# Expert rows of two tables gathered as one row of 8192 bytes, in a hybrid decoder step on one core

## The chip, the core and the metric

One core of a Trainium2 chip (trn2) runs the whole program once. The metric is the device time in microseconds.

## What is computed

One decoder layer for a prompt of 1024 tokens and for 64 sample tokens (8 sequences of 8): norm, one projection, attention over a latent cache (for the samples over 32 pages of 128 rows each), a pooling mixer, a gated merge, and then `peer`, the expert part around which the change turns. All is float32.

```
q = (xt @ peer_w_q).reshape(n_tok, 8, 2, 128)
s = einsum('nhpd,hpkd->nhpk', q, peer_keys)
s_top, i_top = top_k(s, 16)
cand = s_top[..., 0, :, None] + s_top[..., 1, None, :]
best, pos = top_k(cand.reshape(n_tok, 8, 256), 16)
expert = take_along_axis(i_top[..., 0, :, None] * 128 + i_top[..., 1, None, :], pos)
gate = softmax(best)
a = gelu(einsum('td,ted->te', x, peer_u[expert]))
y = einsum('te,ted->td', gate * a, peer_v[expert])
```

Each token has 8 heads of 16 experts; a row of `peer_u` or `peer_v` is 1024 floats.

## The kernel before, in words

The prompt's eight tiles of 128 tokens go through in three groups of 2, 3 and 3 tiles (class `Prompt`); group 0 runs alone, then the other two, the page attention of the samples (class `Pages`, 64 groups of four pages, seven slots each) and the samples' own tail (class `Sample`) run interleaved with the experts. The order on each engine is written out by hand: `Experts` yields one slot at a time on each engine, and `main.to(slot)` runs the generator up to a slot and returns the engine for a piece of other work. There are NU = 1088 slots: 8 tiles of 128 and one half tile (64). `Plan` sets the slots of the prompt's pieces.

`Route` finds the experts of a unit (one head of 32 rows of each of four row groups, 68 units in all): on DVE `top_eight`, `top_sixteen`, `pairs`, `experts` (L1693 to L1757), on ACT the softmax (L1691). A unit is due every 16 slots.

In a slot k, POOL gathers 128 rows of `peer_u` into a ring of 8 tiles (L1820, queue of POOL); DVE multiplies and sums them with the token rows `xrep` (`dot`, L1933), which frees the ring slot. `xrep` holds a token's row on four partition groups; ACT copies it (`replicate`, L1905), five buffers. After 16 dots DVE prepares the gelu (`gelu_in`, L1942 to L1948), ACT takes one tanh (L1916), and DVE makes the weights (L1956) and one 128x512 product, the diagonals of sixteen slots (L1963). Twenty slots after u (LAG), `peer_v` rows are gathered into a ring of 11, in POOL's order behind the `peer_u` gather of that slot, and PE multiplies them with the diagonals into PSUM, four slots at a time (L1891); its last matmul frees the v slots. `collect` (L1974) adds the rest once a tile.

In the page groups PE transposes a page (L2120), ACT copies it (L2216), PE makes keys (L2134), ACT squares them (L2229), DVE sums the squares (L2290) one slot later; `new_maximum` (L2322 to L2328) and `accumulate` (L2338, L2340) keep the running maximum. Of prompt and sample, L1196 is the projection by the peer weights (`in_w_peer`).

What sets the order around the change: DVE's `diagonals` of chunk u stands at slot 16(u+1)+1; PE's matmuls of slots q to q+3 at slot q+23.

Of the kernel before, what the change touches and what calls it, by code (L numbers as in the profile page):

```python
# [14 lines left out]
P = 128  # L15
# [57 lines left out]
TOP = 52400  # L73
# [1583 lines left out]
class Route:  # L1657


    def __init__(self, env, sem):  # L1660
# [56 lines left out]
    def pairs(self):  # L1717
# [16 lines left out]
    def experts(self, dve, u):  # L1734
# [11 lines left out]
        v.tensor_tensor(h4, h4, self.topf.unsqueeze(2).to_broadcast([P, 2, TOPK, TOPK]), ALU.mult)  # L1746
# [13 lines left out]
class Experts:  # L1760


    XBUF = 5

    def __init__(self, env, sem, ps, rt):
# [14 lines left out]
        self.u_at = w  # L1780
        self.u_ring = take(RING, D)
        self.spare = w
        self.v_ring = take(VRING, D)
        self.diag = take(DIAGS, 16, 32)
        self.a, self.a2, self.th, self.wt = take(2, 16), take(16), take(16), take(16)
# [3 lines left out]
        self.u_in, self.v_in = [sem(f"i_u_in{j}") for j in range(RING)], [sem(f"i_v_in{j}") for j in range(VRING)]
        self.u_used, self.v_used = sem("i_u_used"), [sem(f"i_v_used{j}") for j in range(4)]  # L1790
        self.x0_in, self.xt_in, self.x_set, self.h_in = sem("i_x0_in"), sem("i_xt_in"), sem("i_x_set"), sem("i_h_in")
        self.act_in, self.tanh_done, self.diag_done, self.collected = (sem("i_" + n) for n in ("act_in", "tanh", "diag", "collected"))
# [3 lines left out]
        for q in range(NU):  # L1796
            at[q % self.width(q)] += 1
            self.v_count.append(at[q % self.width(q)])
            if q % 128 == 127 or q == NU - 1:
                self.tile_counts.append(tuple(at))  # L1800
# [18 lines left out]
    def gather(self, ring, slot, col, table, done):  # L1819
        self.nc.gpsimd.indirect_dma_start(out=ring[:, slot, :], out_offset=None, in_=self.I[table],  # L1820
                                          in_offset=bass.IndirectOffsetOnAxis(ap=self.ids[:, col:col + 1], axis=0)).then_inc(done[slot], 16)

    def gather_v(self, q):

        w = self.width(q)
        t, r = q // 128, q % 128 // w
        self.gather(self.v_ring, q % VRING, self.column(t, r // TOPK, q % w, r % TOPK), "peer_v", self.v_in)

    def pool(self, pool):
        for k in range(SLOTS):  # L1830
            if k < NU:
                col = self.column(*self.place(k))
                if k == 0:
                    pool.wait_ge(self.sets_used, H + 7)
                if col % TOPK == 0:
                    pool.wait_ge(self.rt.done, col // TOPK + 1)
                if k == 12:
                    pool.wait_ge(self.sets_used, 3 * H)
                    for q in range(VRING):
                        self.gather_v(q)  # L1840
# [831 lines left out]
```

## Time and profile before

| | |
|---|---|
| median of 3 runs | 3795.91 us (3793.19 to 3797.08) |
| profiled execution, span | 3792.2 us |
| instructions | 45054 |
| gathers | 2176, half of `in_peer_u`, half of `in_peer_v` |
| DMA | 1387.36 MB, mean 366 GB/s |

The profiled execution's own time is its span and the start and end around it; of the three runs the nearest, 3793.19 us, lies 1.0 us above the span. The page gives busy time and share of the span by engine; waits and the chain are inferred from semaphores. Times in the rows below are us from the span's start unless marked ns.

### The profile page before, as it was taken

How to read it: one execution, taken by the hardware profiler on the slowest of the kernel's cores; microseconds unless marked ns; L12 is line 12 of the kernel's file. 1: busy time of each engine (PE TensorE's matmuls, PEld its weight loads, DVE VectorE, ACT ScalarE, POOL GpSimd, SP SyncE). 2: the span in 40 equal slices, each digit the busy share in tenths (PEclk: the TensorE clock that was granted, in tenths of full speed). 3: DMA queues.
4: the chain of work that ended last, by engine and by line, in shares of the span. 5: the costliest groups of instructions: out<-in, count | busy, mean ns of one | idle time of the engine just before them, and what ended most of it. 6: DMA issues, size and time to landing. Idle time of an engine off the chain costs nothing.

```text
span 3792.2 us, 45054 instructions
## 1 busy us (share of the span) xinstructions
PE 2995.8 (79%) x13427; PEld 1568.6 (41%) x13427; DVE 2673.4 (70%) x6884; ACT 954.4 (25%) x1899; POOL 2417.9 (64%) x2196
## 2 busy tenths in 40 slices
PE   8998878986797889987688888888888886566345
PEld 5775335533342554443344444444444443423001
DVE  2426887664578876665688988889888987554753
ACT  1211222200123320210245344434453434000100
POOL 0004556764675777665777777777777877666776
PEclk9998978998997889998799999899999998776668
DMA  6456999999999999999999999999999999999999
GB/s 223 109 196 245 334 315 366 412 409 379 368 388 354 382 373 412 409 412 367 382 374 396 390 367 387 373 398 375 385 392 393 375 393 398 413 412 407 409 391 371
DMA packets 434388, 1387.36 MB, mean 366 GB/s; under 512 B 60954, under 2 KB 119291, under 8 KB 429731
## 3 DMA queue, kind: packets, MB, share of 16 engines
q0 software_dynamic: 313344, 1140.99, 77.4%
q1 hardware_dynamic: 120802, 243.49, 18.1%
q8 instruction: 110, 1.80, 0.2%
q14 instruction: 132, 1.07, 0.1%
HBM read 1354.17 MB, written 30.11 MB: 365 GB/s over the span
## 4 chain that ended last, share of the span: by engine, by line
PE 26%; DVE 25%; DMA 20%; POOL 12%; issue 8%; DVEq 4%; ACT 2%; SPq 1%; ACTq 0%; POOLq 0%
POOL arena L1820 12%; DMA arena<-in_peer_v,arena 9%; DVE arena L1933 8%; DMA arena<-in_peer_u,arena 6%; PE ps L1891 5%; PE ps L863 4%; PE ps L2134 3%; PE ps L1196 3%; DVE arena L2290 2%; DMA arena<-in_w_peer 2%; PE ps L813 1%; PE ps L1034 1%; DMA arena<-s_dram 1%; ACT arena L1905 1%; PE ps L1011 1%
## 5 line engine op out<-in xcount | busy, mean ns | idle before, releaser
L1820 POOL DMA_INDIRECT arena<-in_peer_u,arena x1088 | 1215.7, 1117 | 828.7 <-PE ps L1174 300.3
L1933 DVE CUSTOM_DVE_ANT_0 arena<-arena 128x1024 f32<-128x1024 f32 x1088 | 1317.2, 1222 | 444.7 <-DMA arena<-in_peer_u,arena 419.3
L1820 POOL DMA_INDIRECT arena<-in_peer_v,arena x1088 | 1200.7, 1104 | 507.6 <-issue 301.5
L1891 PE MATMUL ps<-arena 128*32 128x512 f32 x4352 | 663.2, 697 | 345.7 <-DMA arena<-in_peer_v,arena 338.8
L2134 PE MATMUL ps<-arena 128*128 128x512 f32 x1056 | 544.6, 640 | 14.9 <-ACT arena L2229 12.9
L1891 PEld LDWEIGHTS ps<-arena 128*32 128x32 f32 x4352 | 141.5, 121 | 713.1 <-issue 706.5
L1196 PE MATMUL ps<-arena 128*128 128x384 f32 (+2 forms) x896 | 250.9, 433 | 53.2 <-DMA arena<-in_w_peer 53.1
L2229 ACT ACTIVATE arena<-ps 128x512 f32<-128x512 f32 x264 | 157.8, 598 | 445.4 <-PE ps L2134 426.8
L2134 PEld LDWEIGHTS ps<-arena 128*128 128x128 f32 x1056 | 191.3, 202 | 177.8 <-issue 167.7
L2142 PEld LDWEIGHTS ps<-arena 128*128 128x128 f32 x1056 | 167.0, 199 | 139.3 <-issue 137.6
L2290 DVE TENSOR_REDUCE arena<-arena 128x8 f32<-128x512 f32 x264 | 180.3, 683 | 49.3 <-ACT arena L2229 37.4
L1196 PEld LDWEIGHTS ps<-arena 128*128 128x128 f32 x896 | 154.8, 199 | 135.7 <-issue 81.1
L2165 PE MATMUL ps<-arena 128*64 128x257 f32 x528 | 140.3, 413 | 65.1 <-ACT arena L2249 65.1
L863 PE MATMUL ps<-arena 128*128 128x384 f32 (+1 forms) x528 | 172.1, 486 | 23.8 <-DVE arena L1452 23.8
L1103 PE MATMUL ps<-arena 128*128 128x384 f32 x512 | 171.5, 489 | 0.0
L2216 ACT ACTIVATE arena<-ps 128x256 f32<-128x256 f32 (+1 forms) x264 | 107.4, 407 | 247.5 <-PE ps L2120 196.8
L2142 PE MATMUL ps<-arena 128*128 128x64 f32 x1056 | 151.9, 268 | 0.0
L1905 ACT ACTIVATE arena<-arena 32x1024 f32<-32x1024 f32 x120 | 126.4, 1053 | 76.5 <-DVE arena L1933 68.3
L863 PEld LDWEIGHTS ps<-arena 128*128 128x128 f32 x528 | 103.5, 198 | 93.3 <-issue 36.9
L2120 PE MATMUL ps<-const,arena 128*128 128x128 f32 x528 | 114.0, 299 | 22.8 <-ACTq L2219 14.9
L1103 PEld LDWEIGHTS ps<-arena 128*128 128x128 f32 x512 | 96.0, 190 | 77.7 <-issue 14.1
L2165 PEld LDWEIGHTS ps<-arena 128*64 128x64 f32 x528 | 71.4, 145 | 117.3 <-ACT arena L2249 77.9
(239 smaller groups left out, 3774.7 us busy)
## 6 DMA issues: line engine op xcount, KB each, us to landing
arena<-in_w_peer SPq DMA_DIRECT2D x64, 576.0 KB, 7.8
arena<-in_w_merge SPq DMA_DIRECT2D x24, 1536.0 KB, 9.5
arena<-in_cache SPq DMA_DIRECT2D x256, 144.0 KB
arena<-in_peer_u,arena POOLq DMA_INDIRECT x1088, 8.5
arena<-in_peer_v,arena POOLq DMA_INDIRECT x1088, 8.7
arena<-in_w_front SPq DMA_DIRECT2D x33, 512.0 KB, 6.7
arena<-in_w_out SPq DMA_DIRECT2D x24, 512.0 KB, 8.9
arena<-s_dram SPq DMA_DIRECT2D x68, 128.0 KB
```

What stands on the lines that cost most here:

```text
L863: last = t.matmul(bank, w[:, k, :], xnT[:, k, :], start=k == 0, stop=k == KD - 1)
L1103: last = t.matmul(ps[:, 2 + 2 * (d % 2) + a, 0:T], ring[:, a * KD + k, :], xnT[:, k, 0:T], start=k == 0, stop=k == KD - 1)
L1196: last = t.matmul(ps[:, 2 + e % 2, lo * P:hi * P], self.p_item(g, j)[:, k, :], xn2T[:, k, lo * P:hi * P], start=k == 0, stop=k == KD - 1)
L1820: self.nc.gpsimd.indirect_dma_start(out=ring[:, slot, :], out_offset=None, in_=self.I[table], in_offset=bass.IndirectOffsetOnAxis(ap=self. ...
L1891: mm = self.nc.tensor.matmul(self.acc[32 * j:32 * j + 32, n, :], self.diag[:, (q0 + j) // 16 % DIAGS, (q0 + j) % 16, :], self.v_ring[:, (q ...
L1905: last = self.nc.scalar.activation(self.xrep[jg % self.XBUF][32 * i:32 * i + 32, :], self.rows[32 * j:32 * j + 32, :], ACT.Copy)
L1933: self.nc.vector.tensor_tensor_reduce(out=u, in0=u, in1=self.xrep[jg % self.XBUF], scale=1.0, scalar=0.0, op0=ALU.mult, op1=ALU.add, accum ...
L2134: last = t.matmul(self.key, self.cTp[:, j % 2, k * P:(k + 1) * P], self.wuk[:, k, :], start=k == 0, stop=k == 1)
L2142: last = t.matmul(out, self.cTp[:, j % 2, k * P:(k + 1) * P], self.qlat[:, k, b * NS:b * NS + NS], start=j + k == 0, stop=False)
L2165: last = self.nc.tensor.matmul(self.acc_ps[0:NS, 0:KL + 1], self.scs[gi % 2][:, j, :], self.source(j, par)[:, 0:KL + 1], start=j == 0, sto ...
L2229: self.nc.scalar.activation(self.sqp[:, j % 2, :], self.key, ACT.Square).then_inc(self.ksq_done, 1)
L2290: self.nc.vector.tensor_reduce(out=self.ssn[:, j, :], in_=self.sqp[:, j % 2, :].rearrange("p (h d) -> p h d", h=H), axis=AX, op=ALU.add).t ...
```

## The change

The two expert tables become one, `in_peer_uv`, with rows of 2048 floats. POOL gathers both halves of an expert at once into one ring of 10 tiles of 2048 (`ring`, `pair_in`); the slot is freed only by PE's matmul. The order of the experts within a tile changes (`place`): four neighbouring slots are now the four row groups. Gelu, tanh and weights are made every four slots (CHUNK), and the diagonals by four ACT copies with a per-partition scale. LAG falls from 20 to 2: PE's matmuls of slots 4c to 4c+3 stand at slot 4c+5, after DVE's weights at 4c+4 and ACT's diagonals at 4c+5. `xrep` has 8 buffers, and ACT fills them 36, 30, 24 and 18 slots ahead. The gathers' descriptor memory shrinks from 16384 to 4096 bytes a partition, which the arena gets. In the route, ids and positions stay whole numbers; the page groups' maximum is one combined product and maximum, kept in two columns in turn. The first ten gathers wait for the prompt's steps whose buffers they overwrite. The samples share semaphores with the prompt.

The changed lines:

```diff
@@ -32,10 +32,11 @@
-RING = 8
-VRING = 11
-DIAGS = 3
-LAG = 20
+GELU_CUBE = 0.044715
+RING = 10
+CHUNK = 4
+DIAGS = 4
+LAG = 2
@@ -70,7 +71,8 @@
-TOP = 52400
+SCRATCH = 4096
+TOP = 52400 + (16384 - SCRATCH) // 4
@@ -1718,10 +1720,8 @@
-        v.tensor_copy(self.topf, self.topi)
-        v.tensor_scalar(self.topf[:, 0, :], self.topf[:, 0, :], float(NK), None, ALU.mult)
@@ -1737,19 +1737,16 @@
-        v.tensor_copy(self.hilof, self.hilo)
-        v.drain()
-        v.tensor_tensor(self.hit, self.hilof.rearrange("p a b -> p (a b)").unsqueeze(2).to_broadcast([P, 2 * TOPK, TOPK]),
+        v.tensor_tensor(self.hit, self.hilo.rearrange("p a b -> p (a b)").unsqueeze(2).to_broadcast([P, 2 * TOPK, TOPK]),
-        v.tensor_tensor(h4, h4, self.topf.unsqueeze(2).to_broadcast([P, 2, TOPK, TOPK]), ALU.mult)
+        v.tensor_tensor(h4, h4, self.topi.unsqueeze(2).to_broadcast([P, 2, TOPK, TOPK]), ALU.mult)
-        v.tensor_tensor(self.ef, self.e2[:, 0, :], self.e2[:, 1, :], ALU.add)
-        v.drain()
-        v.tensor_copy(self.ids[:, u * TOPK:(u + 1) * TOPK], self.ef)
+        v.scalar_tensor_tensor(out=self.ids[:, u * TOPK:(u + 1) * TOPK], in0=self.e2[:, 0, :], scalar=float(NK), in1=self.e2[:, 1, :],
+                               op0=ALU.mult, op1=ALU.add)
@@ -1760,7 +1757,7 @@
-    XBUF = 5
+    XBUF = 8
@@ -1777,26 +1774,24 @@
...
+        self.u_at, self.spare = w, w + 8 * D
+        self.ring = take(RING, 2 * D)
+        self.diag = take(DIAGS, CHUNK, 32)
+        self.a, self.a2, self.th, self.wt = take(2, CHUNK), take(CHUNK), take(CHUNK), take(2, CHUNK)
...
@@ -1808,42 +1803,32 @@
...
+        t, r = k // 128, k % 128
+        return t, r // (TOPK * w), r % w, r % (TOPK * w) // w
...
+    def sets_before(self, k):
+        end = 2 * D * (k + 1)
+        last = min((end - 1) // (9 * P), 6) if end <= 8 * D else min(7 + (end - 8 * D - 1) // (9 * P), 2 * H - 1)
+        return last + 9
...
+                t, m, j, s = self.place(k)
+                col = self.column(t, m, j, s)
+                if k < RING:
+                    pool.wait_ge(self.sets_used, self.sets_before(k))
+                else:
+                    pool.wait_ge(self.v_used[(k - RING) % self.width(k - RING)], self.v_count[k - RING])
+                if s == 0:
...
+                self.nc.gpsimd.indirect_dma_start(out=self.ring[:, k % RING, :], out_offset=None, in_=self.I["peer_uv"],
+                                                  in_offset=bass.IndirectOffsetOnAxis(ap=self.ids[:, col:col + 1], axis=0)).then_inc(self.pair_in[k % RING], 16)
@@ -1876,22 +1860,22 @@
...
+            c, at = divmod(k - LAG, CHUNK)
+            if c >= 0 and at == CHUNK - 1:
+                k0 = c * CHUNK
+                t, r, w = k0 // 128, k0 % 128, self.width(k0)
+                if r == 0:
...
+                pe.wait_ge(self.diag_done, c + 1)
+                for q0 in range(0, CHUNK, w):
+                    for n in range(2):
+                        for j in range(w):
+                            q = q0 + j
+                            mm = self.nc.tensor.matmul(self.acc[32 * j:32 * j + 32, n, :], self.diag[:, c % DIAGS, q, :],
+                                                       self.ring[:, (k0 + q) % RING, D + n * 512:D + (n + 1) * 512],
+                                                       start=r + q0 == 0, stop=r + q0 + w == (128 if t < PT else 64))
+                            if n:
+                                mm.then_inc(self.v_used[j], 1)
@@ -1900,7 +1884,7 @@
-            act.wait_ge(self.u_used, 128 * t0 + 112 + 4 * j0 + 4)
+            act.wait_ge(self.dotted, 128 * t0 + 124 + j0 + 1)
@@ -1909,14 +1893,15 @@
...
+            c, at = divmod(k, CHUNK)
+            if at == CHUNK - 1 and k < NU:
+                act.wait_ge(self.act_in, c + 1)
+                self.nc.scalar.activation(self.th, self.th, ACT.Tanh, scale=0.7978845608028654 * GELU_CUBE).then_inc(self.tanh_done, 1)
+            if at == 1 and 1 <= c <= NU // CHUNK:
+                self.diagonals(act, c - 1)
+            t = (k + 36) // 128
...
+                for j, ahead in enumerate((36, 30, 24, 18)):
@@ -1924,45 +1909,46 @@
...
+        if t and k % 128 < self.width(k):
...
+        dve.wait_ge(self.pair_in[k % RING], 16 * (k // RING + 1))
+        u = self.ring[:, k % RING, 0:D]
...
+                                            accum_out=self.a[:, k // CHUNK % 2, k % CHUNK:k % CHUNK + 1]).then_inc(self.dotted, 1)
...
+        v.scalar_tensor_tensor(out=self.th, in0=self.a2, scalar=1.0 / GELU_CUBE, in1=a, op0=ALU.add, op1=ALU.mult)
...
+        v.scalar_tensor_tensor(out=self.a2.rearrange("p (s j) -> p s j", j=w), in0=a.rearrange("p (s j) -> p s j", j=w), scalar=0.5,
+                               in1=self.gates[:, col:col + TOPK * w].rearrange("p (j s) -> p s j", j=w)[:, s:s + n, :], op0=ALU.mult, op1=ALU.mult)
+    def weights(self, dve, c):
...
+        need(dve, self.diag_done, c - 1)
+        v.scalar_tensor_tensor(out=self.wt[:, c % 2, :], in0=self.th, scalar=1.0, in1=self.a2, op0=ALU.add, op1=ALU.mult).then_inc(self.weights_done, 1)
+    def diagonals(self, act, c):
+        act.wait_ge(self.weights_done, c + 1)
...
+            k0 = CHUNK * (c - DIAGS)
+            for j in range(self.width(k0)):
+                act.wait_ge(self.v_used[j], self.v_count[k0 + CHUNK - self.width(k0) + j])
+        for q in range(CHUNK):
+            last = self.nc.scalar.activation(self.diag[:, c % DIAGS, q, :], self.C["stack"], ACT.Copy, scale=self.wt[:, c % 2, q:q + 1])
+        last.then_inc(self.diag_done, 1)
@@ -1976,13 +1962,13 @@
...
+                if at == CHUNK - 1:
+                    self.gelu_in(c)
+            if at == 0 and 1 <= c <= NU // CHUNK:
+                self.weights(dve, c - 1)
@@ -2241,7 +2228,7 @@
...
+        self.nc.scalar.activation(self.corr, self.m[(gi + 1) % 2], ACT.Exp, bias=self.m[gi % 2], scale=-1.0).then_inc(self.corr_done, 1)
@@ -2319,12 +2306,11 @@
...
+        mnew = self.m[(gi + 1) % 2]
+        v.tensor_tensor_reduce(out=self.held, in0=self.maxT[gi % 2], in1=self.C["ones"][0:NS, :], scale=1.0, scalar=self.m[gi % 2],
+                               op0=ALU.mult, op1=ALU.max, accum_out=mnew)
+        v.drain()
+        v.tensor_scalar(self.diag, self.C["ident"][0:NS, 0:NS], mnew, None, ALU.mult)
@@ -2335,13 +2321,12 @@
-        v.tensor_copy(self.m, self.mnew)
-    def divide(self, dve, b):
+    def divide(self, dve, b, following):
@@ -2650,9 +2636,9 @@
-        "peer_u": A["peer_u"][0], "peer_v": A["peer_v"][0],
+        "peer_uv": np.concatenate([A["peer_u"][0], A["peer_v"][0]], axis=1),
-    nc = bacc.Bacc("TRN2", target_bir_lowering=False, num_devices=1)
+    nc = bacc.Bacc("TRN2", target_bir_lowering=False, num_devices=1, dynamic_dma_scratch_size=SCRATCH)
```

(A line of "..." marks what is left out; removed lines of functions printed above are left out too.) On POOL, 12 gathers of u, 11 of v and then both in turn became 436 gathers of `in_peer_uv`, the memsets of the page groups, and 652 more.

The order on DVE before, beside the page groups, from the gelu's first step (L1942 to L1948) into the route's `experts` (L1737 to L1752):

```order
L1942 TENSOR_TENSOR arena<-arena 128x16
L1944 TENSOR_SCALAR arena<-arena 128x16
L1946 TENSOR_TENSOR arena<-arena 128x16
L1948 SCALAR_TENSOR_TENSOR arena<-arena 128x16
L1737 TENSOR_SCALAR arena<-arena 128x16
L1738 TENSOR_SCALAR arena<-arena 128x16
L1740 CAST arena<-arena 128x32
L1742 TENSOR_TENSOR arena<-arena,const 128x512
L1746 TENSOR_TENSOR arena<-arena 128x512
L1748 TENSOR_REDUCE arena<-arena 128x32
L1750 TENSOR_TENSOR arena<-arena 128x16
L1752 CAST arena<-arena 128x16
```

In it the gelu is 16 wide and comes once in 16 slots; the route makes two casts and one addition around its wide products.

The order on DVE with the change, at the same unit (gelu L1927 to L1931, route L1737 to L1748):

```order
L1927 TENSOR_TENSOR arena<-arena 128x4
L1929 SCALAR_TENSOR_TENSOR arena<-arena 128x4
L1931 SCALAR_TENSOR_TENSOR arena<-arena 128x4
L1737 TENSOR_SCALAR arena<-arena 128x16
L1738 TENSOR_SCALAR arena<-arena 128x16
L1740 TENSOR_TENSOR arena<-arena,const 128x512
L1744 TENSOR_TENSOR arena<-arena 128x512
L1746 TENSOR_REDUCE arena<-arena 128x32
L1748 SCALAR_TENSOR_TENSOR arena<-arena 128x16
```

The gelu is one step shorter, 4 wide and comes every four slots; the casts are gone, and one combined step writes the ids.

The order on ACT before, at a softmax and tanh beside the page groups, with what each row waits for (d_ names are the page groups', i_ the experts', h_ the route's; L2216 copies a page, L2229 squares keys, L1916 is the tanh):

```order
L1691 ACT_TABLE_LOAD [waits h_done]
L1691 ACTIVATE arena<-arena 128x16 [waits h_best]
L1916 ACTIVATE arena<-arena 128x16 [waits i_act_in]
L2216 ACTIVATE arena<-ps 128x256 [waits d_s,d_t_done]
L2229 ACTIVATE arena<-ps 128x512 [waits d_ks,d_key]
L2216 ACTIVATE arena<-ps 128x256 [waits d_s,d_t_done]
```

In sixteen slots this tanh is all that ACT waits for from the experts.

The order on ACT with the change (L2203 copies a page, L2216 squares keys, L1950 are the diagonals):

```order
L2216 ACTIVATE arena<-ps 128x512 [waits d_ks,d_key]
L1950 ACTIVATE arena<-const,arena 128x32 [waits i_v_used2,i_v_used1,i_v_used3,i_v_used0,i_weights]
L1950 ACTIVATE arena<-const,arena 128x32 x3
L2203 ACTIVATE arena<-ps 128x256 [waits d_s,d_t_done]
L2216 ACTIVATE arena<-ps 128x512 [waits d_ks,d_key]
L2203 ACTIVATE arena<-ps 128x256 [waits d_s,d_t_done]
```

The four diagonals wait for DVE's weights, every four slots, and stand ahead of the next page copy and square.

## Rows read from the trace of the kernel before

**Rows 1.** The page: busy time by engine; busy tenths of DMA in 40 slices.

```profile
PE 2995.8 (79%) x13427; PEld 1568.6 (41%) x13427; DVE 2673.4 (70%) x6884; ACT 954.4 (25%) x1899; POOL 2417.9 (64%) x2196
...
DMA  6456999999999999999999999999999999999999
```

**Rows 2.** Stretches, us: engine busy (x instructions), clock, DMA share, GB/s.

```profile
1400.00:1750.00 350.00, 313.02 (x1215) 157.37 (x1208) 219.69 (x540) 43.32 (x72) 237.15 (x216) 0.96 1.03 411
...
1850.00:3140.00 1290.00, 1087.84 (x5144) 548.77 (x5145) 1141.90 (x3073) 561.62 (x1095) 988.45 (x858) 0.95 1.01 384
...
3140.00:3590.00 450.00, 256.18 (x1437) 131.42 (x1435) 272.95 (x681) 53.56 (x110) 313.06 (x292) 0.71 1.03 408
```

**Rows 3.** Groups on DVE, 1850 to 3140: count | busy, mean ns | idle, releaser.

```profile
L1933 DVE CUSTOM_DVE_ANT_0 arena<-arena 128x1024 f32<-128x1024 f32 x430 | 521.8, 1220 | 10.5 <-issue 2.0
...
L2290 DVE TENSOR_REDUCE arena<-arena 128x8 f32<-128x512 f32 x253 | 172.8, 683 | 41.6 <-ACT arena L2229 30.3 <-issue 0.5
```

**Rows 4.** The dots: 311:600, 1100:1400, 600:900, 1400:1750, 3140:3760.

```profile
L1933 DVE CUSTOM_DVE_ANT_0 arena<-arena 128x1024 f32<-128x1024 f32 x78 | 93.8, 1222 | 10.7 <-DMA arena<-in_peer_u,arena 8.1 <-issue 1.6
...
L1933 DVE CUSTOM_DVE_ANT_0 arena<-arena 128x1024 f32<-128x1024 f32 x93 | 111.5, 1219 | 2.3 <-issue 1.8
...
L1933 DVE CUSTOM_DVE_ANT_0 arena<-arena 128x1024 f32<-128x1024 f32 x90 | 109.1, 1224 | 74.2 <-DMA arena<-in_peer_u,arena 72.2 <-issue 1.0
...
L1933 DVE CUSTOM_DVE_ANT_0 arena<-arena 128x1024 f32<-128x1024 f32 x106 | 128.6, 1223 | 95.5 <-DMA arena<-in_peer_u,arena 93.8 <-issue 1.1
...
L1933 DVE CUSTOM_DVE_ANT_0 arena<-arena 128x1024 f32<-128x1024 f32 x210 | 255.3, 1224 | 219.4 <-DMA arena<-in_peer_u,arena 215.0 <-issue 2.4
```

**Rows 5.** The chain of waits, 3140 to 3590, by line.

```profile
by line: DMA arena<-in_peer_v,arena 40.0%; POOL arena L1820 29.3%; issue 11.2%; PE ps L1891 7.1%; DMA arena<-in_peer_u,arena 3.4%; PE ps L2502 3.3%; DVE arena L1933 2.1%; ACT arena L1905 1.3%; PE ps L2134 1.2%; DVE arena L2290 0.3%; ACT L22
```

**Rows 6.** Waits of POOL, 1850 to 3140: us in total, times, longest.

```profile
POOL arena L1820 <- issue: 251.5, 822, 1.0
...
POOL arena L1820 <- DVE arena L1933: 44.1, 28, 3.1
```

**Rows 7.** Timeline of DVE: start us, us, line, operation.

```profile
2621.68 0.08 DVE L1933 DVE_READ_ACCUMULATOR2_ANT arena<- 128x1 f32 x1
...
2622.11 0.17 DVE L1944 TENSOR_SCALAR arena<-arena 128x16 f32<-128x16 f32 x1
...
2622.35 0.17 DVE L1946 TENSOR_TENSOR arena<-arena 128x16 f32<-128x16 f32 x1
...
2622.75 0.17 DVE L1737 TENSOR_SCALAR arena<-arena 128x16 uint32<-128x16 uint32 x1
...
2631.22 0.08 DVE L1933 DVE_READ_ACCUMULATOR2_ANT arena<- 128x1 f32 x1
...
2632.43 0.42 DVE L2333 TENSOR_TENSOR arena<-arena,ps 128x256 f32<-128x256 f32 x1
```

**Rows 8.** Timeline of DVE: first instruction of the maximum, first after it.

```profile
2626.73 0.28 DVE L2322 TENSOR_REDUCE arena<-ps 64x1 f32<-64x128 f32 x1
...
2627.74 0.69 DVE L2290 TENSOR_REDUCE arena<-arena 128x8 f32<-128x512 f32 x1
```

**Rows 9.** Groups on ACT, whole span.

```profile
L1905 ACT ACTIVATE arena<-arena 32x1024 f32<-32x1024 f32 x120 | 126.4, 1053 | 76.5 <-DVE arena L1933 68.3 <-issue 6.9
...
L1916 ACT ACTIVATE arena<-arena 128x16 f32<-128x16 f32 x68 | 14.4, 212 | 414.2 <-DVEq L1947 414.1
```

**Rows 10.** Stretches again, one of 75 us, while merge weights load.

```profile
3270.00:3345.00 75.00, 40.58 (x288) 27.83 (x288) 40.05 (x113) 1.61 (x7) 44.35 (x43) 0.74 1.02 415
```

**Rows 11.** Timeline, all engines, end of the program.

```profile
3760.90 0.21 ACT L1916 ACTIVATE arena<-arena 128x16 f32<-128x16 f32 x1 [40.71 <-DVEq L1947]
...
3765.35 1.91 PE L1891 MATMUL ps<-arena 128*32 128x512 f32 x8 [0.17 <-DMA arena<-in_peer_v,arena]
...
3787.68 1.21 DVE L1974 TENSOR_TENSOR arena<-arena,ps 64x1024 f32<-64x1024 f32 x1 [25.47 <-PE ps L1891]
```

**Rows 12.** Waits of PE, whole span.

```profile
PE ps L1196 <- DMA arena<-in_w_peer: 53.1, 15, 20.4
```

More of the change, by code:

```diff
@@ L1779, in __init__ @@
         self.rows = take(D)
[L1780 to L1785, printed above, removed]
+        self.u_at, self.spare = w, w + 8 * D
+        self.ring = take(RING, 2 * D)
         assert self.spare + 9 * 9 * P <= w
+        self.diag = take(DIAGS, CHUNK, 32)
+        self.a, self.a2, self.th, self.wt = take(2, CHUNK), take(CHUNK), take(CHUNK), take(2, CHUNK)
         self.end = w
         self.acc = ps[:, 0:2, :]
[L1789 to L1792, printed above, removed]
+        self.pair_in, self.v_used = [sem(f"i_pair_in{j}") for j in range(RING)], [sem(f"i_v_used{j}") for j in range(4)]
+        self.dotted, self.x0_in, self.xt_in, self.x_set, self.h_in = (sem("i_" + n) for n in ("dotted", "x0_in", "xt_in", "x_set", "h_in"))
+        self.act_in, self.tanh_done, self.weights_done, self.diag_done, self.collected = (
+            sem("i_" + n) for n in ("act_in", "tanh", "weights", "diag", "collected"))
         self.stored = sem("i_stored")
         self.v_count, at, self.tile_counts = [], [0] * 4, []
[L1796 to L1799, printed above, removed]
+        for k in range(NU):
+            at[k % self.width(k)] += 1
+            self.v_count.append(at[k % self.width(k)])
+            if k % 128 == 127 or k == NU - 1:
                 self.tile_counts.append(tuple(at))
@@ L1817, in column @@
         return (t * 8 + m * (4 if t < PT else 2) + j) * TOPK + s
[L1819 to L1827, printed above, removed]
+    def sets_before(self, k):
+        end = 2 * D * (k + 1)
+        last = min((end - 1) // (9 * P), 6) if end <= 8 * D else min(7 + (end - 8 * D - 1) // (9 * P), 2 * H - 1)
+        return last + 9
     def pool(self, pool):
@@ L1831, in pool @@
             if k < NU:
[L1832 to L1835, printed above, removed]
-                    pool.wait_ge(self.rt.done, col // TOPK + 1)
[L1837 to L1840, printed above, removed]
-                need(pool, self.u_used, k - RING + 1)
-                self.gather(self.u_ring, k % RING, col, "peer_u", self.u_in)
-            q = k - LAG
-            if VRING <= q < NU:
-                pool.wait_ge(self.v_used[(q - VRING) % self.width(q - VRING)], self.v_count[q - VRING])
-                self.gather_v(q)
+                t, m, j, s = self.place(k)
[5 more added lines that the diff above has]
+                if s == 0:
+                    pool.wait_ge(self.rt.done, col // TOPK + 1)
+                self.nc.gpsimd.indirect_dma_start(out=self.ring[:, k % RING, :], out_offset=None, in_=self.I["peer_uv"],
+                                                  in_offset=bass.IndirectOffsetOnAxis(ap=self.ids[:, col:col + 1], axis=0)).then_inc(self.pair_in[k % RING], 16)
             yield
@@ L1857, in sync @@
                 sp.dma_start(self.rows[0:rows], self.env["xn2_dram"][(t + 1) * P:(t + 1) * P + rows, :]).then_inc(self.xt_in, 16)
-            t, r = divmod(k - LAG, 128)
-            if 0 <= t <= PT and r == (112 if t < PT else 40):
+            if t <= PT and r == (112 if t < PT else 40):
                 rows = P if t < PT else NS
@@ L1993, in vector @@
                 rt.experts(dve, EXPERTS_AT[k])
-            t, r = divmod(k - LAG, 128)
-            if 1 <= t <= PT and r == 2:
+            t, r = divmod(k, 128)
+            if 1 <= t <= PT and r == 3:
                 self.collect(dve, t - 1)
@@ L2022, in __init__ @@
         small = take(NS, 8)
-        self.m, self.mnew, self.negm, self.corr, self.gmax, self.rl = (small[:, j:j + 1] for j in range(6))
+        self.m, self.corr, self.rl = [small[:, j:j + 1] for j in range(2)], small[:, 2:3], small[:, 3:4]
+        self.held = take(NS, P)
         self.diag, self.acc, self.lat = take(NS, NS), take(NS, KL + 1), take(NS, KL)
```

91 lines of the change are left out of this document (19 added, 72 removed).

## The prediction

> **What bounds the kernel now.** I read the page first, then the stretches, the waits of each engine in them, and the chain. The page names no engine as the bound: PE is busy 79%, DVE 70%, POOL 64% of the span, while the DMA digits stand at 9 from the seventh slice on [rows 1]. The stretches say more [rows 2]. A slot is one gathered expert (k), 1088 of them. From 1400 to 1750 and from 3140 on the DMA engines are full and move 408 to 411 GB/s. From 1850 to 3140, where the page groups run beside the experts, they move 384 although their share reads 1.01: nearly busy, not at their best rate. DVE is busy there for 1142 of 1290 us, and not once idle for a gather: it waits 30.3 us for ACT and no `in_peer_u` stands behind its dots [rows 3]. So DVE sets the pace there: 430 dots in 1290 us, 3.00 us a slot. Two prompt stretches look alike (78 dots in 311 to 600, 93 in 1100 to 1400, with 8.1 and 0 us of waiting for gathers); in three others (90, 106 and 210 dots) DVE stood 72, 94 and 215 us waiting for `in_peer_u` [rows 4]: there the transfers set the pace. The chain through 3140 to 3590 says the same, 40% DMA of `in_peer_v` and 29% POOL [rows 5].
>
> POOL is near the edge: from 1850 to 3140 it is busy 988 us and loses 251.5 us between instructions for nothing that the profile shows, 1240 of 1290 us, and waits only 44.1 us for a slot of the ring [rows 2, 6].
>
> **The change, part by part.** The sum is made against the profiled span, 3792.2 us; the median of the three runs is 3.7 us above it.
>
> *Expert arithmetic on DVE.* Before, sixteen slots pay once: from the accumulator read at 2621.68 to the next other work at 2622.75 is 1.07 us, and from 2631.22 to 2632.43 1.21 us for weight and diagonal [rows 7]. That is 2.28/16 = 0.143 us a slot. After, every four slots pay: the first block less one step (2622.11 to 2622.35, 0.25 us), so 0.82, and of the second only drain and weight, about 0.27 (0.18 until the weight starts, 0.1 until the next). 1.09/4 = 0.273. DVE gets 0.130 us more a slot.
>
> *Route.* A unit (16 slots) loses two casts, the doubling and one addition. Three of these steps stood alone between drains; at 0.25 us each, 0.75 us a unit, 0.047 a slot.
>
> *Maximum of the page groups.* Four instructions from 2626.73 to 2627.74 (1.01 us [rows 8]) become two; I take off one step and the negation, 0.3 us a group of seven slots (between 0 and 0.5).
>
> Over 1850 to 3140: 430 × 0.130 = +56; 27 units × 0.75 = -20; 61 groups × 0.3 = -18. DVE +18 us. In the two prompt stretches where DVE (or PE beside it) paces: 171 × (0.130 - 0.047) = +14.
>
> *The handover.* The four copies that make a diagonal go to ACT, 0.21 us each by its nearest row, the tanh of a tile of 16 columns [rows 9]; four are 0.85. PE may start four slots' matmuls only after DVE's weights and those copies: some 1.2 us after the dot of the slot before. Before, PE had six slots of slack. The order shows that ACT now stands at `i_weights` ahead of the copies and squares that the page keys need. No row shows this wait. Its ends are 0 and 1.2 us × 107 = 128 us in that stretch. I take 8 us, near the lower end, because PE there is idle 202 of 1290 us [rows 2], 1.9 us a handover, and since ACT is mostly early: it stood 414 us waiting for DVE before 53 of 68 tanhs [rows 9].
>
> *Replicas.* Eight buffers in place of five let ACT copy rows 36 to 18 slots ahead. ACT stood 68.3 us for dots there [rows 9], 4.2 us of copying behind each. Of that I count 9 us on the path (0 to 30).
>
> *Transfers.* The bytes are the same: 1.049 MB a slot. In the full stretches gathers of 4096-byte rows are nearly all that moves, at 408 to 411 GB/s [rows 2]; in 3270 to 3345, with the merge weights' rows of 12288 bytes among them, 415 [rows 10]. So 2.557 us (at 410) becomes 2.527: 406 slots × 0.031 = -13 us (0 to -25). The Trainium skill (DMA: Bandwidth & Descriptors, Rules for kernel authors) wants at least 1 MiB a DMA for bandwidth. By its fit (Anatomy of one DMA: 2.0 us plus the bytes at 436 GB/s) a pair of half-megabyte gathers would cost 6.4 us and one gather 4.4, and the change would save 2 us in every slot; this trace does not agree, a pair costs 2.6 us already, because the fixed part of one lies under the next.
>
> *POOL.* 1088 fewer gathers at 1.1 us. It hides where DVE or DMA paces. What it gives is a ring that is full when the pages end: at most 2.8 MB more in flight at 3140, 7 us.
>
> *The end.* The lag between u and v, twenty slots, goes. Their 10 MB move into 1850 to 3140, which has (410 - 384) × 1290 us = 33 MB to spare. From the last tanh (3760.90) to the end are now 31.3 us; after, tanh 0.2, weights 0.3, diagonals 0.9, two groups of 1.91 us on PE and the 4.5 us from the last addition to the end [rows 11], 9.7 us. -21 us.
>
> *At nothing:* the ids read as whole numbers in the 512-wide products (same width), the shared semaphores, the smaller descriptor memory (ten gathers at most are out), a table load ahead of most tanhs (their total stays, and they stand before the wait, not after it).
>
> Sum: +18 + 14 + 8 - 9 - 13 - 7 - 21 = **-10 us**, so 3782 for the profiled execution and 3786 as a median, 0.26% faster. A measurement of this kernel can tell 0.2%, 7.6 us.
>
> **The rivals.**
>
> *Handover on the path, slower.* The diagonals on ACT and the four-slot step tie DVE, ACT and PE in one ring: DVE's weights, ACT's copies, PE, the next page key, ACT's square, DVE's reduction. For it: DVE already waits 27 times for that square [rows 3]; PE had been free to run ahead of the dots. Against it: PE's idle share. With half of the 1.2 us uncovered it costs 64 - 8 = +56, 3842; it decides from 0.24 us a handover, where the total passes +7.6. Chance 0.27.
>
> *POOL was the pace of the pages, faster.* If its 1240 us of work were what held 1290, the stretch would shrink to DVE's own work and more: -50 us, 3736. For it: its waits for a slot are only 44 us [rows 6]. Against: no dot waits for a gather there. Chance 0.20.
>
> *Weights starve, slower.* Where the prompt's loads share the engines with gathers, each of whose pieces is now twice as long, they land later. PE waits 53.1 us in 15 cases for `in_w_peer` now [rows 12]; doubled, +53, 3839. The Trainium skill (DMA: Bandwidth & Descriptors, Queues, rings and completion order; SWDGE vs HWDGE vs iDMA) has an engine change between queues at packet boundaries, with packets preferably of 4096 bytes at most. That speaks for this rival; the trace has no gather above 4096 to test it. Chance 0.05.
>
> *It doesn't do what it says.* Rows of 8192 bytes cut in two again, or the small descriptor memory holding POOL up: a gather costs POOL 2.2 + 0.3 us, still under 3.00, and the transfers gain nothing: -10 + 13 = +3, at most some 10 more. 3799. Chance 0.08.
>
> **How the numbers follow.** The forecast has 0.40, with its own range 3750 to 3815 from the bounds above (transfers, replicas, the maximum, 0.3 us a handover): of it 0.22 fall over 7.6 us faster, 0.12 within, 0.06 slower. With the rivals: faster 0.22 + 0.20 + 0.02 = 0.44; same 0.12 + 0.04 = 0.16; slower 0.06 + 0.27 + 0.05 + 0.02 = 0.40. Both signs are nearly even. The range 3727 to 3862 takes in the gain by POOL and the handover at some 0.7 of its price, and leaves out its worst end and a doubled gain by POOL.
>
> **What would show it.** Right: 1850 to 3140 (or its like) about as long as now, DVE still without waits for the gathers, its small steps four times as many and the 512-wide diagonal gone; POOL busy near a third; 412 to 416 GB/s in the full stretches; under 12 us from the last dot to the end. The handover rival would show as DVE idle before the page reductions or the weights, and PE idle before its expert matmuls with ACT named. The POOL rival: a slot of 2.87 us there. Wrong altogether: gathers of over 2 us on POOL, or a transfer rate under 405 where nothing else paces.

## The result: slower, and the profile after

The changed kernel takes 4026.03 us (median of 4 runs, 4023.51 to 4029.11) beside 3796.49 us for the kernel before (4 runs, 3793.19 to 3797.30): a ratio of 1.0612, 95% interval 1.0598 to 1.0625. That is 6.1% slower, outside my range. The profiled execution took 4029.11 us, its span is 4027.3 us.

The page of the changed kernel, busy time, DMA digits and GB/s by slice, the gathers' queue, and three groups of its fifth part:

```profile
PE 3094.0 (77%) x13427; PEld 1586.5 (39%) x13427; DVE 2701.1 (67%) x7164; ACT 1232.3 (31%) x3195; POOL 1210.5 (30%) x1108
...
DMA  6558978998898899998779988998989898989998
GB/s 214 149 172 316 353 287 361 420 397 343 342 400 329 301 380 421 402 384 330 285 301 353 367 341 332 356 356 344 347 340 355 333 362 349 397 368 414 411 404 363
...
q0 software_dynamic: 156672, 1140.92, 71.2%
...
L1830 POOL DMA_INDIRECT arena<-in_peer_uv,arena x1088 | 1209.0, 1111 | 2787.2 <-PE ps L1874 2213.7
...
L1874 PE MATMUL ps<-arena 128*32 128x512 f32 x4352 | 732.2, 759 | 496.9 <-ACT arena L1950 496.8
...
L1950 ACT ACTIVATE arena<-const,arena 128x32 f32<-128x32 f32 x1088 | 259.0, 309 | 348.1 <-DVE arena L1940 344.3
```

The change does what it says: 1088 gathers at 1.11 us on POOL, and 156,672 packets, 144 a gather, where 256 or more would mean rows cut in two. DVE has 28 us more work, ACT 278 us more. PE reads 98 us more for the same 13427 matmuls, and its mean granted clock in the stretch below is 0.92 where it was 0.95 [rows 2]. No engine is busier than 77%, and the DMA digits, 9 nearly throughout before [rows 1], now swing between 7 and 9.

The stretch of the page groups (slots 440 to 881), its counterpart [rows 2], then DVE's waits and PE's and POOL's longest wait in it (us, times, longest):

```profile
1950.00:3380.00 1430.00, 1119.83 (x5108) 539.92 (x5109) 1130.97 (x3072) 663.86 (x1595) 469.35 (x425) 0.92 0.89 344
```

```profile
POOL arena L1830 <- PE ps L1874: 866.5, 107, 14.0
...
DVE arena L2277 <- ACT arena L2216: 116.0, 50, 5.3
...
DVE arena L2292 <- ACT arena L2227: 52.1, 29, 5.1
...
DVE arena L1918 <- issue: 1.5, 9, 0.2
...
PE ps L1874 <- ACT arena L1950: 202.6, 106, 6.8
```

PE stands 202.6 us ahead of the expert matmuls (L1874) for ACT's copies (L1950). DVE does not wait for the gathers; it waits 168 us for ACT's squares (L2216) and roots (L2227), where it had waited 30.3 for squares [rows 3] and 17.2 for roots. POOL waits for the matmul that frees a pair. The kernel before, 1850 to 3140, PE's largest wait and DVE's wait for roots:

```profile
PE ps L2153 <- DVE arena L2317: 79.6, 38, 5.1
...
DVE arena L2305 <- ACT arena L2240: 17.2, 9, 3.9
```

There PE waited most for DVE, at the end of the page chain: it had run ahead. In the changed kernel the same wait (L2140 for L2304) is 26.6 us. How PE's wait for the copies reaches DVE stands in the timeline of one place (start us, us, line, operation, idle before):

```profile
2612.04 0.16 DVE L1940 SCALAR_TENSOR_TENSOR arena<-arena 128x4 f32<-128x4 f32 x1 [0.16 <-issue]
...
2612.24 0.96 ACT L1950 ACTIVATE arena<-const,arena 128x32 f32<-128x32 f32 x4 [1.14 <-DVE arena L1940]
...
2613.34 1.92 PE L1874 MATMUL ps<-arena 128*32 128x512 f32 x16 [2.47 <-ACT arena L1950]
...
2615.49 1.89 POOL L1830 DMA_INDIRECT arena<-in_peer_uv,arena  x1 [5.82 <-PE ps L1874]
2615.58 1.89 PE L2121 MATMUL ps<-arena 128*128 128x512 f32 x4
...
2617.50 0.60 ACT L2216 ACTIVATE arena<-ps 128x512 f32<-128x512 f32 x1 [1.23 <-PE ps L2121]
...
2618.13 0.69 DVE L2277 TENSOR_REDUCE arena<-arena 128x8 f32<-128x512 f32 x1 [1.56 <-ACT arena L2216]
```

Weights at 2612.04, copies, PE's matmuls after 2.47 us idle, only then the page's keys, ACT's square, and DVE's reduction after 1.56 us idle. PE cannot get ahead of DVE any more, so the page work that DVE needs from PE comes late. The gather that those matmuls release starts at 2615.49, after POOL stood 5.82 us.

Where the time goes, by the start of the dot of a slot (us from the span's start, one profiled execution each; e7 and e11 stay within 16 us of the changed kernel at every slot):

| kernel | k 0 | k 440 | k 881 | end | 0 to 440 | 440 to 881 (pages) | 881 to end |
|---|---|---|---|---|---|---|---|
| before | 334 | 1817 | 3151 | 3792 | 1483 | 1334 | 641 |
| changed | 328 | 1898 | 3404 | 4027 | 1570 | 1506 | 623 |
| e1 ring of 8 | 328 | 2049 | 3585 | 4307 | 1721 | 1536 | 722 |
| e8 six x buffers, ring of 11 | 330 | 1880 | 3378 | 3999 | 1550 | 1498 | 621 |
| e6 two gathers a pair | 330 | 1906 | 3399 | 4060 | 1577 | 1492 | 662 |
| e2 diagonals on DVE | 333 | 1899 | 3374 | 3999 | 1566 | 1475 | 625 |
| e3 LAG 4 | 328 | 1982 | 3390 | 4025 | 1654 | 1408 | 635 |
| e4 light before | 330 | 1797 | 3112 | 3763 | 1467 | 1315 | 651 |
| e5 two rings | 330 | 1848 | 3337 | 3960 | 1518 | 1489 | 623 |
| e13 two rings, LAG 4 | 326 | 1832 | 3166 | 3792 | 1506 | 1334 | 626 |
| e10 light, deeper rings | 329 | 1793 | 3102 | 3747 | 1464 | 1309 | 645 |
| e9 two rings, LAG 6 | 332 | 1839 | 3190 | 3812 | 1507 | 1351 | 622 |
| e12 pair ring, best | 332 | 1919 | 3317 | 3933 | 1587 | 1398 | 616 |
| e14 pair ring, LAG 6 | 329 | 2385 | 4359 | 5064 | 2056 | 1974 | 705 |

The change loses 172 us in the pages and 87 in the prompt groups, and gains 18 after them.

### The profile page after: what moved, and what is told of

It reads as the page before. It is cut to its first block, busy times and chain, and to the rows that moved or that the text cites. A ratio compares the mean times of both kernels' runs of the same rounds, so it can differ in the third digit from the quotient of the medians.

```text
span 4027.3 us, 46204 instructions
## 1 busy us (share of the span) xinstructions
PE 3094.0 (77%) x13427; PEld 1586.5 (39%) x13427; DVE 2701.1 (67%) x7164; ACT 1232.3 (31%) x3195; POOL 1210.5 (30%) x1108
## 3 DMA queue, kind: packets, MB, share of 16 engines
q0 software_dynamic: 156672, 1140.92, 71.2%
## 4 chain that ended last, share of the span: by engine, by line
PE 36%; DVE 21%; DMA 19%; issue 7%; ACT 6%; DVEq 6%; POOL 2%; SPq 1%; ACTq 0%; POOLq 0%
DMA arena<-in_peer_uv,arena 12%; PE ps L1874 11%; DVE arena L1918 7%; PE ps L2121 5%; PE ps L1198 4%; PE ps L865 3%; DMA arena<-in_w_peer 2%; ACT arena L1950 2%; DVE arena L2277 2%; POOL arena L1830 2%; DVEq L1937 2%; ACT arena L1889 2%; DVEq L1926 1%; PE ps L815 1%; PE ps L1036 1%
## 5 line engine op out<-in xcount | busy, mean ns | idle before, releaser
L1830 POOL DMA_INDIRECT arena<-in_peer_uv,arena x1088 | 1209.0, 1111 | 2787.2 <-PE ps L1874 2213.7
L1918 DVE CUSTOM_DVE_ANT_0 arena<-arena 128x1024 f32<-128x1024 f32 x1088 | 1323.0, 1221 | 435.7 <-DMA arena<-in_peer_uv,arena 410.7
L1874 PE MATMUL ps<-arena 128*32 128x512 f32 x4352 | 732.2, 759 | 496.9 <-ACT arena L1950 496.8
L2121 PE MATMUL ps<-arena 128*128 128x512 f32 x1056 | 529.6, 624 | 26.0 <-ACT arena L2216 22.4
L1874 PEld LDWEIGHTS ps<-arena 128*32 128x32 f32 x4352 | 144.4, 128 | 899.3 <-ACT arena L1950 561.9
L1950 ACT ACTIVATE arena<-const,arena 128x32 f32<-128x32 f32 x1088 | 259.0, 309 | 348.1 <-DVE arena L1940 344.3
L1899 ACT ACTIVATE arena<-arena 128x4 f32<-128x4 f32 x272 | 55.5, 204 | 933.0 <-DVEq L1930 931.9
L1198 PE MATMUL ps<-arena 128*128 128x384 f32 (+2 forms) x896 | 254.5, 438 | 67.3 <-DMA arena<-in_w_peer 66.2
L2216 ACT ACTIVATE arena<-ps 128x512 f32<-128x512 f32 x264 | 157.9, 598 | 369.6 <-PE ps L2121 363.4
L2203 ACT ACTIVATE arena<-ps 128x256 f32<-128x256 f32 (+1 forms) x264 | 106.8, 405 | 254.3 <-PE ps L2107 190.8
```

The costliest lines, as they stand in the source:

```text
L1198: last = t.matmul(ps[:, 2 + e % 2, lo * P:hi * P], self.p_item(g, j)[:, k, :], xn2T[:, k, lo * P:hi * P], start=k == 0, stop=k == KD - 1)
L1830: self.nc.gpsimd.indirect_dma_start(out=self.ring[:, k % RING, :], out_offset=None, in_=self.I["peer_uv"], in_offset=bass.IndirectOffsetOn ...
L1874: mm = self.nc.tensor.matmul(self.acc[32 * j:32 * j + 32, n, :], self.diag[:, c % DIAGS, q, :], self.ring[:, (k0 + q) % RING, D + n * 512: ...
L1918: self.nc.vector.tensor_tensor_reduce(out=u, in0=u, in1=self.xrep[jg % self.XBUF], scale=1.0, scalar=0.0, op0=ALU.mult, op1=ALU.add, accum ...
L1950: last = self.nc.scalar.activation(self.diag[:, c % DIAGS, q, :], self.C["stack"], ACT.Copy, scale=self.wt[:, c % 2, q:q + 1])
L2121: last = t.matmul(self.key, self.cTp[:, j % 2, k * P:(k + 1) * P], self.wuk[:, k, :], start=k == 0, stop=k == 1)
```

## The experiments

Each kernel is the changed one with one edit, unless said otherwise. Two theories at first. A, *the ring*: a pair keeps its 8 KB a row until the weighted product, so few gathers are under way. B, *the tie*: PE stands in its order for the diagonals, and what is queued behind it comes late. Then C (chunks of four cost by themselves), D (the 8 KB packets) and D2 (the small descriptor memory). The kernels ran in groups (e1 to e4, e5 to e8, e9 to e12, e13 and e14), the changed kernel apart from them, and the kernel before ran beside each. Its median lay between 3786.92 and 3796.49 us, so up to some 10 us between kernels of different groups say nothing. The ratios are to the kernel before of the same group; differences in us between groups are of the medians as they stand. e4, e5, e9 and e10 have four runs, e13 has ten, the others two.

**e1.** `RING = 10` to `RING = 8`, with `take(2, 2 * D)` behind the ring so that nothing else moves.

> The changed kernel (4026 us) with a ring of 8 pairs instead of 10, its memory otherwise laid out the same. Theory A (the ring is too short: a pair keeps its 8 KB a row until the weighted product, and four are freed at once): two fewer gathers under way cost a lot, 4150 us or more, with POOL's wait for the weighted product and the dots' wait for in_peer_uv both up. Theory B (what costs is the diagonals' handover over ScalarE, in order with the page copies): the ring is deep enough, under 4070 us.

4311.88 us, ratio to before 1.1365 (1.1342 to 1.1388): 286 us for two pairs, as A has it. DVE's and POOL's waits:

```profile
POOL arena L1831 <- PE ps L1875: 2504.0, 275, 26.5
...
DVE arena L1919 <- DMA arena<-in_peer_uv,arena: 862.3, 527, 9.4
```

DVE's wait for gathers was 410.7 us in the changed kernel. But of the 280 us of span only 30 fall in the pages; there the ring is not what decides most.

**e2.** The diagonals on DVE, behind the weights; `need(dve, self.diag_done, c - 1)` and ACT's `diagonals` go:

```diff
+        v.drain()
+        v.tensor_tensor(self.diag[:, c % DIAGS, :, :], self.C["stack"].unsqueeze(1).to_broadcast([P, CHUNK, 32]),
+                        self.wt[:, c % 2, :].unsqueeze(2).to_broadcast([P, CHUNK, 32]), ALU.mult).then_inc(self.diag_done, 1)
```

> The changed kernel with the four diagonals of a chunk made by one VectorE product of 128x(4x32) right behind the weights, no ScalarE copies (1088 of 309 ns) and no hop. Theory B: PE's wait for the copies (497 us in all) goes, most of the loss comes back, under 3900 us. Theory A: the slot is freed only about 1 us sooner, VectorE gets some 272 x 0.3 = 80 us more work; 3960 to 4060 us.

4002.01 us, 1.0548 (1.0527 to 1.0569): 24 us, inside A's range and not in B's. PE now waits 369.8 us for DVE's product in place of 496.8 for ACT's copies. B as I had put it, that most of the loss is the hop over ACT, falls. But the run does not weigh the hop alone: the products put 79.5 us of work on DVE, with 67.9 us idle before them. In the pages (1950 to 3350) DVE's waits for squares and roots fell from 168 to 82 us and PE's for the handover from 202.6 to 107.0, while the stretch became only 31 us shorter. The hop may be up to half of the tie. The rest is PE's place in the order: slot 4c+5 comes right behind DVE's weights at slot 4c+4, whoever makes the diagonals.

**e3.** `LAG = 2` to `LAG = 4`: PE's product at slot 4c+7.

> The changed kernel with the weighted product two slots later in PE's order (LAG 4 instead of 2), nothing else. Theory B: PE no longer stands waiting for the copies ahead of page work, 3900 to 3990 us. Theory A: pairs are freed up to two slots later, as with a shorter ring: over 4080 us and more waits for in_peer_uv.

4017.55 us, 1.0589 (1.0560 to 1.0619), from two runs 18 us apart, so the 8 us under the changed kernel are no gain clear of noise. Outside both expectations, and the stretches say why: the pages are 98 us shorter and the prompt groups 84 longer. Both theories hold, each in its own stretch, and LAG trades one for the other. Here the product alone moved, and no gather with it. DVE's waits in e3's pages, 2000 to 3380:

```profile
DVE arena L1918 <- DMA arena<-in_peer_uv,arena: 69.0, 68, 2.5
...
DVE arena L2277 <- ACT arena L2216: 15.2, 19, 2.6
DVE arena L2292 <- ACT arena L2227: 6.5, 8, 1.8
```

**e4.** The kernel before with only the lighter route, page maximum and gelu cube of the diff.

> The kernel before (3796 us) with only the lighter arithmetic: route, page maximum, and the gelu cube in one instruction; both rings, both tables and 16-slot chunks as before. If VectorE sets the page stretch as I said: 20 + 18 + some 68 x 0.1 = 45 us less VectorE work, two thirds of it on the path, 3760 to 3785 us. Rival (POOL's issue sets that stretch): 3790 to 3800 us.

3764.73 us, 0.9923 (0.9906 to 0.9939), faster by 30 us, as expected if DVE sets the pace. Nineteen of them fall in the pages, where I had said some 38 of DVE's work.

**e5.** The 20,480 words split again: 8 slots of u, freed by the dot, 12 of v, freed by the product; all else as changed.

```diff
-                    pool.wait_ge(self.v_used[(k - RING) % self.width(k - RING)], self.v_count[k - RING])
+                    pool.wait_ge(self.dotted, k - RING + 1)
...
+            q = k - 1
+            if 0 <= q < NU:
...
+                    pool.wait_ge(self.v_used[(q - VRING) % self.width(q - VRING)], self.v_count[q - VRING])
+                self.gather(self.v_ring, q % VRING, self.column(*self.place(q)), "peer_v", self.v_in)
```

> The changed kernel with its 20,480 words of ring split again: 8 slots of u freed by the dot, 12 slots of v freed by the weighted product, two tables and 2176 gathers of 4 KB a row; chunks of four, ScalarE's diagonals and all else as changed. Theory A (the pair is held too long): the loss goes, 3760 to 3840 us. Theory C (chunks of four with their hops cost by themselves, whatever the ring): over 3950 us.

3953.12 us, 1.0429 (1.0402 to 1.0455): by the number theory C, not A. The ring as joined costs 73 us (69 by the ratios), 52 of them in the prompt groups. The pages stay long, 1489, with the same waits (PE 210.0 us for ACT's copies, DVE 118.3 for squares and 52.2 for roots), which leaves the tie or C; e9 tells them apart.

**e6.** Two gathers of 4 KB a row into the halves of the same pair, `for h, table in enumerate(("peer_u", "peer_v"))`.

> The changed kernel with each pair fetched by two gathers of 4 KB a row from two tables into the halves of the same ring of 10, both awaited by the dot. Only the packet size and POOL's count of gathers go back. Theory A: the ring stays the limit and the transfers get a little slower, 4026 to 4110 us. Theory D (the 8 KB packets are what hurts): under 3950 us.

4064.22 us, 1.0726 (1.0693 to 1.0760). The joint row is worth 38 us to this ring; D falls. All of it lies behind slot 881 (662 us for 623); the pages are not longer. The run gives back the packets and POOL's 1088 gathers together and does not part the two. The Trainium skill (DMA: Bandwidth & Descriptors, SWDGE vs HWDGE vs iDMA) prefers packets of 4096 bytes at most; this pair of kernels does not agree, the gathers in packets of 8192 bytes give the shorter time.

**e7, e8.** `XBUF = 6`, the last two replicas of a tile at `(36, 30, 2, 1)`, and the rows of h loaded 17 slots later; in e8 also `RING = 11`.

> Control for the next: six buffers of replicated rows instead of eight, the last two replicas of a tile made at its edge; ring of 10. All theories: some us more at each of eight tile edges, 4030 to 4090 us.

> The same with the freed 2048 words as an eleventh pair. Theory A, by the slope of 143 us a pair from 8 to 10, less as it flattens: 60 to 140 us under its control. Theory B: within 20 us of its control.

e7: 4018.75 us, 1.0606 (1.0574 to 1.0639), under the 4030 to 4090 expected and no more than with eight buffers (4026): that the last two replicas of a tile are early is worth nothing here. e8: 3999.06, 1.0554 (1.0522 to 1.0587), 20 us under its control, at the edge of B's range. The ring's price is steep from 8 to 10 and flat after; neither of my two expectations had both. In the prompt groups too the two pairs gave 151 us and the eleventh 20 under the ring of ten (1721, 1570, 1550). That the tie takes over there is my reading, and no run shows it.

**e9.** e5 with `LAG = 6`, the v gathers at `q = k - 5`, `collect` at `r == 7`.

> The two rings of e5 (3953 us) with the weighted product at slot 4c+9 instead of 4c+5 and the v gathers, and the tile's last sum, four slots later too. The ring lets go of as much as before; only the tie in order PE, ScalarE, VectorE is loosened. Theory B in the page stretch (VectorE waited there 114 us for squares and 52 us for roots, both behind PE's wait for the copies): the page stretch (slots 440 to 881) falls from 1489 to about 1380 us, the whole to 3800 to 3860 us, some 50 us above e4 for the chunks of four. If the small steps of four cost the time themselves: over 3920 us.

3814.40 us, 1.0066 (1.0049 to 1.0083), as B has it: 139 us from the later product, with the v gathers and the tile's last sum moved along with it. No run with two rings moves the product alone; e3, which does so with pairs, takes DVE's waits in the pages down as far (22 us; 40 here). C falls, but for the 50 us over e4.

**e10.** e4 with `SCRATCH = 4096`, `RING = 9`, `VRING = 13` (and the diff's shared semaphores).

> e4 (lighter arithmetic on the kernel before, 3765 us) with the descriptor memory at 4096 bytes and the words it frees given to the rings: 9 of u and 13 of v instead of 8 and 11. If transfers still run dry at times: 10 to 30 us less than e4, 3735 to 3755 us. If the rings of the kernel before were long enough: within 8 us of e4. If the small descriptor memory holds POOL back: more than e4 by 10 us or over.

3747.43 us, 0.9887 (0.9869 to 0.9905): 17 us under e4 (14 by the ratios, since the groups differ), and the fastest kernel here.

**e11.** `SCRATCH = 6144` in the changed kernel.

> The changed kernel with 6144 bytes of descriptor memory instead of 4096, nothing else. Theory D2 (the small descriptor memory holds the gathers back): 30 us or more off 4026. Theories A and B: within 10 us of it.

4023.39 us, 1.0614 (1.0592 to 1.0637), the changed kernel's time. D2 falls.

**e12.** e8 with the diagonals of e2 and LAG 4.

> The pair ring at its best by the runs so far: eleven pairs (x buffers 6), diagonals on VectorE, the weighted product two slots later (LAG 4). By the parts: 4026 less 24 (diagonals), 9 (lag), 20 (eleventh pair), 7 (x buffers) is 3966 us. If the parts help each other (a later product no longer starves the ring when the pair is freed sooner): 3900 to 3940 us. In no theory under the kernel before.

3931.30 us, 1.0371 (1.0347 to 1.0396): 35 us better than the parts added. The best of the pair rings tried stays 133 us behind two rings with LAG 4.

**e13.** e5 with `LAG = 4` and `q = k - 3`.

> The two rings of e5 with the weighted product at slot 4c+7 (LAG 4), the v gathers two slots later: the fourth cell of the square of ring (pair, two) by LAG (2, 4). If the two costs are tied through the pair ring: LAG 4 gives 9 us there but over 100 us here, 3810 to 3850 us. If they are separate and simply add: 9 us less than e5, 3940 us.

3798.52 us (10 runs, 3794.22 to 3813.26), 1.0025 (1.0012 to 1.0037): 155 us less than e5, better than I expected. DVE's waits in the pages of e5 (1850 to 3330) and of e13 (1850 to 3150), and PE's for the copies:

```profile
PE ps L1887 <- ACT arena L1963: 210.0, 106, 11.1
...
DVE arena L2290 <- ACT arena L2229: 118.3, 51, 5.8
DVE arena L2305 <- ACT arena L2240: 52.2, 27, 5.5
```

```profile
DVE arena L2290 <- ACT arena L2229: 12.7, 14, 2.6
DVE arena L2305 <- ACT arena L2240: 6.5, 7, 1.8
...
PE ps L1887 <- ACT arena L1963: 4.2, 2, 2.3
```

151 us of DVE's waiting go, and the pages shorten by 155 (1489 to 1334). PE is ahead again: it waits 56.6 us for DVE at the end of the page chain (L2153 for L2317), 25.1 in e5.

**e14.** The changed kernel with `LAG = 6` and `collect` at `r == 7`.

> The changed kernel with the weighted product at slot 4c+9 (LAG 6), ring of 10 pairs. A pair is then held four slots longer than at LAG 2, and one to four gathers are under way instead of five to eight. Ring theory: much as the ring of 8 or worse, 4200 to 4500 us, VectorE's wait for in_peer_uv over 1000 us though PE's wait for the copies is gone. If the tie were all: under 4000 us.

5061.91 us, 1.3345 (1.3313 to 1.3377): the right direction and far too low a price. DVE waits 1800.8 us for `in_peer_uv`. With the product of chunk c at slot 4c+9, the pair of slot 4c+10 can only be asked for after that, so a chunk would pay the whole way: issue, transfer and landing, dot, product. That is read from the order of slots, not traced. 4735 us from the first dot to the end, over 272 chunks, are 17.4 us a chunk.

The square of ring by LAG, in us:

| | LAG 2 | LAG 4 |
|---|---|---|
| pairs, 10 | 4026 | 4018 |
| two rings, 8 and 12 | 3953 | 3799 |

With two rings the later product (and its gathers) gives 155 us, with pairs 8, which is within the spread of e3's two runs. From before to the changed kernel the steps are: lighter arithmetic -30 (3794, the median of before in its group, to e4), chunks of four with ACT's diagonals +34 (e4 to e13, which also differ in buffers, descriptor memory and the order of experts), the product two slots behind its chunk +155 (e13 to e5), the rings joined +73 (e5 to changed, where 38 are already won back by the joint row). By the ratios the four are -29, +39, +153 and +69.

## Why the prediction was wrong

**The step that failed is *The handover*, taken at +8 us; the runs show 155 us (e5 against e13).** My forecast of 3786 us rested on it. The hops were sized nearly right: four copies 0.85 us said, 0.96 measured; some 1.2 us from weights to PE, 1.3 in the timeline. What I priced was the wrong thing. PE's wait is not the hop but PE's *lead*: how far it would have been ahead of DVE. I named "six slots of slack" before and did not ask what they bought: in the pages PE used them to bring keys early enough for DVE's sums. My argument from PE's idle time (202 us, 1.9 a handover) was no argument. That time was no spare room in front of the products: 79.6 us of it were PE waiting for DVE at the end of the page chain, the sign of its lead. In the changed kernel PE waits 202.6 us in 106 cases, again 1.9 us each, but this wait stands in front of the page's keys, and DVE, which sets the pace, waits at the end of that chain. The upper end, 128 us in that stretch, was too low as well: from e13 to e5 DVE's waits there grow by 151 us and the stretch by 155.

**The second mechanism is in no step.** I counted "ten gathers at most are out" and set *POOL* to -7 for a fuller ring. A pair is held from its gather to the product, so when DVE is at slot k, gathers can be issued to k+5 to k+8, less while PE is late. In the traces it is less: at the start of a dot in the pages 4.0 gathers beyond it had left POOL in the mean, 2.1 with the ring of 8 and 3.0 with LAG 4, where the kernel before had 4.9 of u. Before, u slots came free at each dot, and a row of v was fetched only twenty slots after its u, when its weights were due. That costs 73 us net (e5), 52 in the prompt groups, and with ten pairs it keeps a later product from helping (e3, e14).

**The rivals.** *Handover on the path* had the mechanism, the whole chain, and its marks in the profile (DVE idle before the page reductions, PE idle before the expert matmuls with ACT named); its 3842 us was too small, since it priced half of the hop, where the whole lead was lost, and had nothing of the ring. *POOL was the pace* is not borne out: e4 and e10, with POOL's 2176 gathers unchanged, have pages 19 and 25 us shorter than before. The changed kernel itself says nothing on it, since something else holds its pages. *Weights starve* is real but small: PE waits 66.2 us in 16 cases for `in_w_peer`, 13 more than before [rows 12]; in e6, with rows of 4096 bytes again, it waits 40.9 us in 11 cases, and that kernel is still 38 us slower. *Doesn't do what it says* fell with the page and e11.

**The other terms.**

*Expert arithmetic*: four small groups on DVE in the pages, 106 each, are 69 us busy and 49 idle before them, 1.11 us a chunk for 1.09 said. Their effect on the length is smaller: e13's pages are 19 us longer than e4's, where I had +56. *Route* and *maximum*: from its first instruction to the next work the maximum fell from 1.01 us [rows 8] to 0.79, and a copy of 0.14 us (L2338) went, 0.36 in all for my 0.3, yet e4's pages gained 19 us for 38. DVE sets the pace there less strictly than I said. *Replicas*: ACT's idle time before them went from 76.5 to 2.0 us. What that alone is worth no run shows, since e7 keeps the first two replicas early and has 2.3. *The end*: 9.7 us said from the last tanh, 9.9 measured (4017.42 to 4027.3). *Transfers*: undersized, and misread: from 1400 to 1750 the gathers were 111.33 of 143.80 MB, not nearly all. Stretches in which they are all that moves, the first in the kernel before, the second in the changed one:

```profile
3680.00:3760.00 80.00, 39.44 (x126) 8.38 (x122) 41.33 (x72) 0.22 (x1) 60.78 (x64) 0.84 1.03 409
```

```profile
3920.00:4000.00 80.00, 46.26 (x128) 9.53 (x128) 44.73 (x96) 9.04 (x40) 35.99 (x33) 0.75 1.01 421
```

421 GB/s is 2.49 us a slot and 409 is 2.56, 0.07 less, where I had 0.031. With merge weights among them it is 422 (3520 to 3600) for 415 [rows 10]. It came in few stretches, since the DMA engines are rarely full now.

What stays open: why e14 is so much dearer than the step from 10 to 8 pairs, when in the pages it has 1.7 gathers beyond the dot in the mean and e1 has 2.1; how much of the 34 us from e4 to e13 is DVE's small steps and how much ACT's copies; how much of the tie is the hop; and whether PE's longer matmuls add to the loss or only follow from its waits. In the pages the products read 726 ns each, 619 with LAG 4 (e3).

## What to carry to other kernels

An in-order engine's wait costs what is queued behind it, not what the hop takes: before moving work closer to its producer, ask which engine used the slack, and follow its next output to the engine that sets the pace. When two buffers with different release points are joined, the pair is held to the later one; count the gathers that can be under way at the moment the consumer stands at slot k, not the slots of the ring. And a change of many parts can hide a good one: the lighter arithmetic and the words from the descriptor memory, without the joined ring, gave the fastest kernel, 1.1% under the one before.

## What the runs showed of the hardware

Where gathers alone filled the DMA engines, rows of 8192 bytes moved at 421 GB/s (3920 to 4000), rows of 4096 at 409 in the kernel before (3680 to 3760). A gather costs POOL much the same for either: 1.11 us, before 1.10 and 1.12. Four ACT copies of 128x32 read 309 ns each in the groups but 0.96 us for the four in the timeline (259.0 us for all 1088): one after the other they overlap, so four cost less than four times one. A reduction with a running maximum in one instruction took 0.34 us and 0.07 for its read, the plain reduction it replaced 0.28 [rows 8]. Descriptor memory of 4096 and of 6144 bytes a partition made no difference to this ring of gathers (4026 and 4023 us).
